# A two-layer hybrid trunk on one core: two-head attention groups with a summed output projection, unit-stride dense norms, and a projection chunk ahead of W1

## The reference, cut to what matters

```python
for i in range(DEPTH):                       # DEPTH = 2
    h = rms_norm(x, norm_mix_g[i])
    mix = s5_mixer(h, ...) if i % 2 == 0 else diff_attention(h, ...)
    x = x + mix
    x = x + hier_moe(rms_norm(x, norm_ffn_g[i]), ...)
return rms_norm(x, final_norm_g)
# diff_attention: 8 heads, two softmaxes a head
p = softmax(where(mask, q @ k.T, -inf))
attn = p[:, :, 0] - lam * p[:, :, 1]
o = attn @ v                                  # 128 wide a head
o = o * rsqrt(mean(o * o) + EPS) * subln_g * (1 - lambda_init)
return o.reshape(256, 1024) @ w_o
```

## Time and profile before

| what | value |
|---|---|
| time, median of 3 runs (lowest to highest) | 883.79 us (882.64 to 884.89) |
| profiled execution: time, span | 885.29 us, 882.9 us |
| PE busy | 740.7 us (84%) |
| DVE, ACT, POOL busy | 260.9, 189.9, 52.3 us |
| memory read and written | 236.32 MB; 424 GB/s where the loads stream without a pause |
| front (to the gated output) / layer 1 MoE / norm and projections / attention / layer 2 MoE | 0 to 165 / to 402 / to 511 / to 591 / to 883 us |

### The profile page before, as it was taken

One profiled execution on the slowest core, in us unless ns is written; L12 is line 12 of the kernel. 1 busy time (PEld: TensorE's weight loads), 2 busy tenths in 40 slices (PEclk: granted clock), 3 DMA queues, 4 the chain that ended last, 5 costly groups with the idle time before them and its releaser, 6 DMA issues.

```text
span 882.9 us, 15820 instructions
## 1 busy us (share of the span) xinstructions
PE 740.7 (84%) x6435; PEld 444.1 (50%) x6435; DVE 260.9 (30%) x747; ACT 189.9 (22%) x440; POOL 52.3 (6%) x52
## 2 busy tenths in 40 slices
PE   5797899889958766767999957598988999988796
PEld 4696555565524333344444434266545555544453
DVE  7958962161101101103215341315111121111112
ACT  4574513241100000003013241214110111100012
POOL 4693000000000000000000000000000000000000
PEclk9899899879998979888999977797999999998898
DMA  9624218668999999999805640042699940899991
GB/s 249 174 75 139 75 50 358 280 265 332 424 423 424 424 425 423 423 413 391 315 1 191 226 155 1 0 165 121 270 422 426 416 183 0 325 424 425 422 399 54
DMA packets 58157, 236.32 MB, mean 268 GB/s; under 512 B 18216, under 2 KB 18416, under 8 KB 33520
## 3 DMA queue, kind: packets, MB, share of 16 engines
q1 hardware_dynamic: 57216, 235.24, 67.1%
q10 hardware_dynamic: 880, 0.23, 0.1%
HBM read 234.41 MB, written 1.05 MB: 267 GB/s over the span
## 4 chain that ended last, share of the span: by engine, by line
PE 58%; SPq 16%; DMA 11%; DVE 10%; ACT 3%; issue 2%; ACTq 0%; DVEq 0%
SPq L402 14%; PE ps L1674 10%; PE ps L1739 10%; DMA ring<-in_moe_w_down 7%; PE ps L1592 6%; PE ps L1709 6%; PE ps L1716 5%; PE ps L1656 4%; PE ps L1804 4%; DMA work<-in_moe_w_down 3%; SPq L400 2%; PE ps L1463 2%; PE ps L1433 2%; PE ps L1623 1%; PE ps L1784 1%
## 5 line engine op out<-in xcount | busy, mean ns | idle before, releaser
L1674 PE MATMUL ps<-ring,work 128*32 128x256 f32 x1600 | 118.3, 430 | 37.1 <-DMA ring<-in_moe_w_up 25.3
L1674 PEld LDWEIGHTS ps<-ring,work 128*32 128x32 f32 x1600 | 65.2, 123 | 82.9 <-issue 61.2
L1273 DVE TENSOR_TENSOR work<-ps,work 128x256 f32<-128x256 f32 x21 | 12.9, 616 | 292.9 <-PE ps L1674 292.9
L1674 PE MATMUL ps<-work 128*32 128x256 f32 x992 | 79.3, 405 | 17.2 <-DMA work<-in_moe_w_up 9.6
L1709 PE MATMUL ps<-ring,work 128*32 128x512 f32 x512 | 70.8, 610 | 9.2 <-DMA ring<-in_moe_w_down 6.5
L1716 PE MATMUL ps<-work 128*128 128x512 f32 x168 | 77.7, 605 | 0.0
L1656 PE MATMUL ps<-work,xr 128*128 128x128 bf16 x736 | 68.2, 222 | 2.2 <-DVE work L1223 2.2
L1674 PEld LDWEIGHTS ps<-work 128*32 128x32 f32 x992 | 42.7, 117 | 51.9 <-issue 29.4
L1656 PE MATMUL ps<-work 128*128 128x128 bf16 x368 | 65.5, 222 | 0.0
L1656 PEld LDWEIGHTS ps<-work,xr 128*128 128x128 bf16 x736 | 57.6, 99 | 12.7 <-issue 8.6
L1739 PE MATMUL ps<-ring,hT 128*128 128x512 f32 x128 | 58.1, 609 | 1.7 <-ACT hT L555 1.7
(11 more groups left out here) (308 smaller groups left out, 951.8 us busy)
## 6 DMA issues: line engine op xcount, KB each, us to landing
ring<-in_moe_w_gate SPq DMA_DIRECT2D x24, 2048.0 KB, 24.5
ring<-in_moe_w_down SPq DMA_DIRECT2D x23, 2048.0 KB, 21.2
work<-in_moe_w_up SPq DMA_DIRECT2D x15, 2048.0 KB, 22.8
ring<-in_moe_w_up SPq DMA_DIRECT2D x15, 2048.0 KB, 23.1
work<-in_moe_w_down SPq DMA_DIRECT2D x8, 2048.0 KB, 27.6
work<-in_moe_w_gate SPq DMA_DIRECT2D x7, 2048.0 KB, 20.0
ring<-in_ssm_w_glu SPq DMA_DIRECT2D x4, 2048.0 KB, 8.9
ring<-in_attn_w_qkv SPq DMA_DIRECT2D x4, 2048.0 KB, 26.8
```

Source lines behind the costliest of these rows:

```text
L1674: ins = mm(ps[s, 6 + j // 2, 0:256], xg[:, k, s], pairs[slots[e // 2]][e % 2][:, k, :], start=(k == 0), stop=(k == KD - 1))
```

## The change

It does four things.
- Dense norms: `turn(i)` reads x with unit stride; the gains of the two dense norms and the dense weights are loaded in the matching order. The first gain is now loaded in 4-byte pieces on ScalarE's queue instead of SyncE's.
- Front: the four clears of `part(8192, 4096)` go from GpSimd to ScalarE (as a copy times zero). `stack_by(0)` goes ahead of ScalarE's wait for B. TensorE does `inputs(4)` ahead of `turn_w1(0, 0)`, and all later chunks one place sooner.
- Attention: output norm, turn and projection of half 1 go by the group of two heads (`var_o`, `norm_o`, `turn_o`, `out_add`). `out_add(g)` multiplies two heads by both chunks of w_o and sums over the groups in banks 2 and 3.
- Attention's order: the projections of half 0 (`out_proj(0)`, `out_proj(1)`) stand between the groups of half 1, the rest as the order below shows.

```diff
@@ sync
-            sp.dma_start(gq[:, 0, :], a["norm_mix_g"][0].rearrange("(q k) -> q k", k=KD)).then_inc(s_gain0, 16)
-            columns(0, a["ssm_w_in"][0], 0, True)
+            columns(0, a["ssm_w_in"][0], 0, False)
...
@@ gpsimd
-            pool.wait_ge(normed, 2)
-            clear(part(8192, 4096), 4)
             pool.wait_ge(hT_psum, 1)
             clear(bb1, 1)
...
+            pool.wait_ge(rest_clear, 1)
@@ scalar
+            dma(gq[:, 0, :], a["norm_mix_g"][0].rearrange("(k q) -> q k", k=KD), s_gain0)
             dma(drep[0:8, :], a["ssm_d"][0].rearrange("(c p) -> c p", p=P), s_d)
...
+            for n in range(4):
+                ins = act.activation(part(8192 + 1024 * n, 1024), con[:, 0:1024], ACT.Copy, scale=0.0)
+            ins.then_inc(rest_clear, 1)
...
+            act.wait_ge(normed, 2)
+            stack_by(0, range(16))
             act.wait_ge(bbar_ready, 1)
...
             first(0)
             first(1)
-            act.wait_ge(normed, 2)
-            stack_by(0, range(16))
             keep_w1T(0, 0)
...
             soft(2)
+            keep_oT(0)
+            keep_oT(1)
             soft(3)
...
@@ vector
+            var_o(0)
             norm_o(0)
             peak(2)
             peak(3)
             combine(2)
+            add_mix(0, 7)
+            combine(3)
+            var_o(1)
             peak(4)
-            combine(3)
-            add_mix(0, 5)
+            combine(4)
+            var_o(2)
             peak(5)
-            combine(4)
+            norm_o(1)
+            norm_o(2)
             add_mix(1, 5)
             combine(5)
+            var_o(3)
             var_tile(3, 0)
-            norm_o(1)
+            norm_o(3)
             norm_tile(3, 0)
+            var_o(4)
+            norm_o(4)
...
@@ tensor
-                            ins = mm(ps[:, (4 if i else 0) + b, 256 * (k % 2) + P * tt:256 * (k % 2) + P * tt + P], by_k(tt)[:, k, :],
+                            ins = mm(ps[:, (4 if i else 0) + b, 256 * (k % 2) + P * tt:256 * (k % 2) + P * tt + P], x[:, tt, P * k:P * k + P],
                                      scales[:, tt, :], start=True, stop=True)
...
             for c in range(1, 4):
                 inputs(c)
+            inputs(4)
             turn_w1(0, 0)
-            inputs(4)
+            inputs(5)
             turn_w1(0, 1)
...
+            def out_add(g):
+                h0 = 2 * (g - 2)
+                pe.wait_ge(exp_ready, exps[3])
+                pe.wait_ge(oT_ready, g + 1)
+                for c in range(2):
+                    for k in (h0, h0 + 1):
+                        ins = mm(ps[:, 2 + c, :], oT[:, k, P:2 * P], win[slot_of(unit(0, NQ, 6 + c))][:, k, :],
+                                 start=(k == 0), stop=(k == KD - 1))
+                    if g == 5:
+                        ins.then_inc(wo_done, 1)
```

More of the change, by code:

```diff
@@ L468, in _ @@
                 if c < 6:
-                    columns(unit(0, NQ, c), a["attn_w_qkv"][0], 512 * c, True)
+                    columns(unit(0, NQ, c), a["attn_w_qkv"][0], 512 * c, False)
                 else:
@@ L617, in _, with stack_by @@
                                    ACT.Copy, scale=(-1.0 if i else 1.0)).then_inc(c_ready, 1)
+            def stack_by(b, ns):
+                act.wait_ge(u_done, 2 * b + 2)
+                for n in ns:
+                    stack(act.copy, b, n).then_inc(u4_ready, 1)
+            act.wait_ge(normed, 2)
+            stack_by(0, range(16))
             act.wait_ge(bbar_ready, 1)
-            act.wait_ge(cleared, 6)
+            act.wait_ge(cleared, 5)
             for i in range(2):
@@ L658, in own @@
                         act.copy(dst[:, :, r, 32 * (3 - j):P], kps[:, :, 0:32 * (j + 1)]).then_inc(f_ready, 1)
-            def stack_by(b, ns):
-                act.wait_ge(u_done, 2 * b + 2)
-                for n in ns:
-                    stack(act.copy, b, n).then_inc(u4_ready, 1)
             first(0)
             first(1)
-            act.wait_ge(normed, 2)
-            stack_by(0, range(16))
             keep_w1T(0, 0)
@@ L813, in keep_att, with keep_o, root_o, keep_oT @@
                 act.copy(atT[:, g % 2, :], ps[:, groups[g][4], :]).then_inc(attT_ready, 1)
-            def keep_o(n):
-                act.wait_ge(av_done, (1, 2, 4, 6)[n])
-                act.copy(osb[n // 2][:, 512 * (n % 2):512 * (n % 2) + 512], ps[:, (7, 7, 6, 7)[n], :]).then_inc(osq, 1)
-            def root_o(b):
-                act.wait_ge(ovar, b + 1)
-                act.activation(asm[:, 32 + 8 * b:40 + 8 * b], asm[:, 16 + 8 * b:24 + 8 * b], ACT.Sqrt).then_inc(oroot, 1)
-            def keep_oT(b, c, bank):
-                act.wait_ge(o_turned, 2 * b + c + 1)
-                act.copy(oT[:, 4 * c:4 * c + 4, b * P:(b + 1) * P],
-                         ps[:, bank, :].rearrange("p (h t) -> p h t", h=4)).then_inc(oT_ready, 1)
+            def keep_o(g):
+                act.wait_ge(av_done, g + 1)
+                if g < 2:
+                    dst = osb[0][:, 512 * g:512 * g + 512]
+                else:
+                    dst = osb[1][:, 256 * (g - 2):256 * (g - 2) + 256]
+                act.copy(dst, ps[:, groups[g][5], 0:512 if g < 2 else 256]).then_inc(osq, 1)
+            def root_o(n):
+                c0, c1 = (0, 8) if n == 0 else (8 + 2 * n - 2, 8 + 2 * n)
+                act.wait_ge(ovar, n + 1)
+                act.activation(oroots[:, c0:c1], ovars[:, c0:c1], ACT.Sqrt).then_inc(oroot, 1)
+            def keep_oT(n):
+                act.wait_ge(o_turned, n + 1)
+                if n < 2:
+                    dst, src = oT[:, 4 * n:4 * n + 4, 0:P], ps[:, 5 - n, :]
+                else:
+                    dst, src = oT[:, 2 * n - 4:2 * n - 2, P:2 * P], ps[:, 4, 0:2 * P]
+                act.copy(dst, src.rearrange("p (h t) -> p h t", t=P)).then_inc(oT_ready, 1)
             for c in range(4):
@@ L843, in _ @@
             soft(2)
+            keep_oT(0)
+            keep_oT(1)
             soft(3)
             keep_att(2)
[L847 removed]
+            keep_o(2)
+            keep_att(3)
             soft(4)
[L849 to L851 removed]
+            keep_o(3)
             soft(5)
+            root_o(1)
+            root_o(2)
             keep_att(4)
[L854 to L860 removed]
+            keep_o(4)
+            keep_oT(2)
+            square_tile(0, 6)
+            root_o(3)
+            root_tile(3, 0)
+            keep_att(5)
+            keep_o(5)
+            keep_oT(3)
+            root_o(4)
+            keep_oT(4)
+            keep_oT(5)
             keep_tile(3, 0)
@@ L1786, in values, with turn_o, out_proj @@
                 ins.then_inc(av_done, 1)
-            def turn_o(b, c, bank):
-                pe.wait_ge(o_ready, b + 1)
-                if b == 0 and c == 1:
-                    pe.wait_ge(oT_ready, 1)
-                for h in range(4):
-                    ins = pe.transpose(ps[:, bank, P * h:P * h + P], osb[b][:, 512 * c + P * h:512 * c + P * h + P], ident)
+            def turn_o(n):
+                pe.wait_ge(o_ready, max(n, 1))
+                src = osb[0][:, 512 * n:512 * n + 512] if n < 2 else osb[1][:, 256 * (n - 2):256 * (n - 2) + 256]
+                for h in range(src.shape[1] // P):
+                    ins = pe.transpose(ps[:, 5 if n == 0 else 4, P * h:P * h + P], src[:, P * h:P * h + P], ident)
                 ins.then_inc(o_turned, 1)
-            def out_proj(n, bank):
-                b, c = n // 2, n % 2
+            def out_proj(c, bank):
                 slot = slot_of(unit(0, NQ, 6 + c))
                 pe.wait_ge(*landing(unit(0, NQ, 6 + c)))
-                pe.wait_ge(oT_ready, 2 * b + 2)
-                if n:
-                    pe.wait_ge(mixed, 4 + min(n, 2))
+                pe.wait_ge(oT_ready, 2)
                 for k in range(KD):
-                    ins = mm(ps[:, bank, :], oT[:, k, b * P:(b + 1) * P], win[slot][:, k, :],
-                             start=(k == 0), stop=(k == KD - 1))
+                    ins = mm(ps[:, bank, :], oT[:, k, 0:P], win[slot][:, k, :], start=(k == 0), stop=(k == KD - 1))
                 ins.then_inc(wo_done, 1)
+            def out_add(g):
[8 more added lines that the diff above has]
+                        ins.then_inc(wo_done, 1)
             pe.wait_ge(hT_ready, 6)
```

82 lines of the change are left out of this document (42 added, 40 removed).

## The result

The changed kernel takes 857.1 us (median of 4 runs, 855.65 to 860.56), beside 883.2 for the kernel before in the same job: ratio 0.9701, 95% interval 0.9678 to 0.9724. That is 26 us less; 30.7 were forecast. The profiled execution has a span of 855.0 us for 882.9.

A forecast was written before the change was run, and what follows sets the result against it. The prediction took waits for both MoE weight streams, released by TensorE's expert passes, as the bound, so savings ahead arrive whole: 7.0 + 2.1 + 21.6 = 30.7 us off the median 883.79 gives 853.1, range 847 to 863.

The forecast's parts named there:

- Streams: Both MoE weight streams start from TensorE events, so they keep their length and shift by 7 and 31 us.
- Term 3: Attention after the projections: output projections placed inside the softmax and split by head pairs save 21.6 us (15 to 24).
- Term 2: Turn of layer 2's norm: unit-stride weight loads save 2.1 us (0 to 4.0).
- Term 1: Front, 0 to 98 us: moved memsets and an earlier input chunk bring the second drive 7.0 us sooner (3.5 to 8.5).
- From there to 98 us the chain is VectorE's scan alone: Front, after the second drive's start: only VectorE's scan sets the time, so the 7.0 us saved arrive whole.
- the sentence on GpSimd's W2: Front: GpSimd's W2 products start 2.4 us sooner too and stay ahead of the taps.
- (b): Rival: half clock in projection 1, the partial projections or the second drive gives back 6 to 12 us, 859 to 865; 0.14.
- The turn of layer 1 [...] is waited for by nobody on this chain: 0: Front: unit-stride weights in the turn of layer 1's norm gain 0, as nothing on the chain waits for it.
- the 2.4 us that every new time was moved by: Front: gain on VectorE's parameter chain from moving four GpSimd memsets to ScalarE, taken as 2.4 of 2.2 to 3.1 us.
- (a): Rival: the first gain, in 4-byte pieces, lands late and delays the sines and VectorE by 2 to 4 us, 855 to 857; 0.12.
- (d): Rival: 336 ns loads not from the stride, 3.28 us row not GpSimd's doing; front 4.6, norm's turn 0, 857.6 us; 0.08.
- (c): Rival: half clock through the whole attention and the turns behind it makes the kernel slower, 888 us; 0.02.

The follow-up runs named there:

- attn_only: The kernel before with only the attention's part of the change; 861.2 us, ratio 0.9747.
- scores_ahead: The changed kernel with group 4's scores, maxima and exponentials moved ahead, the scores before the first output projection; 850.0 us, ratio 0.9632.
- norm_only: The kernel before with only the unit-stride dense norms and weight loads, the first gain on ScalarE's queue; 880.7 us, ratio 0.9961.
- short_products: stack_ahead with the last quarter of GpSimd's W2 products left out (wrong output, a test only); 850.5 us, ratio 0.9636.
- stack_ahead: The changed kernel with VectorE's eight stack copies ahead of its last weights and the second drive ahead of W1's sixth turn; 855.4 us, ratio 0.9682.
- front_only: The kernel before with only the front's part: memsets to ScalarE, its stack copies and an input chunk moved ahead, gain loaded as before; 882.2 us, ratio 0.9991.
- gain_first: The changed kernel with layer 1's gain, still in 4-byte pieces, issued first on SyncE's queue ahead of the projection's weights; 854.2 us, ratio 0.9672.

## Why the prediction was right, and where it was not

The forecast was 853.1 in a range of 847 to 863; 857.1 is in it, and faster was given 0.97. The attention and the streams were right by their mechanism. The front was not, and 857.1 lies just outside the 849 to 857 that had 0.64: the front gave 5.5 us too little ahead of the first stream, and what lies between the streams 2.0 too much, which hid part of it.

**Streams.** Right: both as long as before, shifted by 1.5 and 27.3 us.

**Term 3, the attention.** Right: 20.9 us in the full change, 22.4 in attn_only, for 21.6 laid out. The wait for group 4's exponentials was forecast as 1.6 us and is 1.93, and projection 0 with its half clock as 8.7 and is 8.66. Projection 1 was laid out at full clock, 6.9, and took 8.16. What the order cost by queueing group 4's maxima behind VectorE's add was seen, and scores_ahead shows that it could be had back with more.

**Term 2, the turn.** The mechanism was right, the size too small: 3.3 us for 2.1, 3.4 in all in norm_only. Strided weight loads took 336 ns at either clock; unit-stride ones went down to 192 at full clock, but their median in this turn was 333, as it ran mostly at half. What I left out is that the projections behind the turn lose their dip of the clock too (14.00 us for 15.7), which is half of the term.

**Term 1, the front.** Wrong: 1.3 us at the GLU for 7.0. The step that failed is "From there to 98 us the chain is VectorE's scan alone", together with the sentence on GpSimd's W2, which I only held against the taps that use it. In the changed kernel the missing 5.7 us are 2.1 of a later second drive (60.42 for 58.3), 1.9 of its half clock (rival (b)) and 1.7 of the first step beside GpSimd (3.5 us for 1.8). But the table shows that the first two count for little: whether the second drive comes at 58 or at 62, the scan gets through its first step only when GpSimd's products end. They end only 0.8 us sooner than before, since GpSimd starts them behind VectorE's powers, and these come 0.9 sooner (29.18 for 30.10), where 2.4 was forecast. short_products shows it as a cause: against stack_ahead, with a quarter of the products left out and nothing else changed, it gives 4.2 us at the GLU.

A second step failed ahead of it: "The turn of layer 1 [...] is waited for by nobody on this chain: 0", and with it the 2.4 us that every new time was moved by. VectorE copies out that turn's banks in the middle of its parameters. front_only, which keeps the strided turn, gained 0.25 us there; gain_first gained 2.0. In the changed kernel the late gain then took part of it back: its fourth turn ended at 53.2 for 51.4, and the first drive of gain_first comes 0.7 us sooner. So the 2.1 us are the late gain in part only.

I had read the lock-out of one VectorE row by GpSimd and didn't ask where else the two engines meet once the schedule has moved. In the kernel before, GpSimd's last product ends as the scan's first row starts (69.88 and 69.92), so nothing there is slow to be seen.

**The rivals.** (a) came true by its mechanism (landing at 14.4), but it cost the front 1 to 2 us at the GLU, so that the result near its 855 to 857 is due to it only in part. (d) with its 857.6 fits by luck: both its conditions were false, since the scalar row did fall to 0.21 and the loads to 192 ns at full clock. (b) happened in the second drive, where most of it was covered, and in projection 1 for 1.1 us (8.16 for 7.06 in scores_ahead), far from the 6 to 12 that it named. (c) did not occur.

## What to carry to other kernels

Before the front of a chain is moved forward, ask beside which work of other engines its rows will run at their new times: two rows that don't meet before the change can lock each other out after it, and the trace of before shows no trace of it. An engine that delivers in time can still be the bound, if the critical engine's rows don't run beside its own; leaving out a part of its work is a cheap test. A row that is freed pays only up to the next wait of its engine: look for that wait before counting the gain. And a wait ahead of a long run of matmuls can cost twice, by itself and by the clock behind it (8.66 us behind 3.06 of idling, 7.08 where work was put into it), so such work can pay more than its own time.

## What the runs showed of the hardware

- VectorE's products with both inputs in SBUF, 128 to 256 elements wide, took 1.0 to 1.4 us beside GpSimd's products in place of 0.28 to 0.42; one got through for each GpSimd instruction. Rows with an input in PSUM were unharmed (VectorE's W1 products of 128x384, 0.54 to 0.56 us in every row, all of them beside GpSimd's). Beside GpSimd's memsets the two-input rows ran at full speed, but a TENSOR_SCALAR of 32x128 was held (0.49 to 3.28 us for 0.21). The Trainium skill ("SBUF — State Buffer", Who interferes with whom) says the first: a VectorE instruction with two SBUF inputs contends with a GpSimd instruction that reads SBUF, not with one that only writes it. The traces agree. By that page, which I had not weighed, the collision could have been foreseen.
- The 1024 pieces of 4 bytes took 12.3 us to land as the fourth load of ScalarE's queue, issued together with SyncE's load of 2 MB, and 5.8 as the fourth of SyncE's, 0.5 us ahead of it; 128 pieces of 32 bytes took 6.5 on ScalarE's queue and 6.1 on SyncE's.
- A weight load of 128x128 with a stride of 8 floats took 336 ns at a granted 0.58 and at 1.00. A unit-stride one took 186 at its shortest (norm_only), and 333 in the rows of layer 2's turn at a granted 0.50. It also took 333 in some 20 of the first loads of layer 1's turn (9.6 to 13.9 us of the changed kernel), where the profile shows a granted 1.00, and 192 behind them. Why these were slow stays open.
